# A down-projection with its operands turned around: tokens stationary, W2 moved in rows of 512 columns

## What is computed

```python
def swiglu(h, w1, w3, w2):
    return (jax.nn.silu(h @ w1) * (h @ w3)) @ w2      # D_FF = 2816, D_MODEL = 1024

h = modulate(rms_norm(x, g_ffn2[i]), sh3, sc3)
x = x + 0.5 * (1.0 + gt3[:, None, :]) * swiglu(h, w1_ffn2[i], w3_ffn2[i], w2_ffn2[i])
return rms_norm(x, g_final)
```

## Time and profile before

| | us |
|---|---|
| median of three runs | 1112.61 |
| the profiled execution's own time | 1113.34 |
| its span | 1111.5 |
| PE busy | 1095.6 |
| DVE busy | 689.1 |
| ACT busy | 583.0 |
| second down-projection, first to last matmul's start | 980.65 to 1104.00 |

### The profile page before, as it was taken

How to read it: one execution, slowest core, us unless ns; L and a number is a source line. 1 busy time by engine, 2 the same in 40 slices (tenths; PEclk the granted TensorE clock), 3 DMA queues, 4 the chain that set the end, 5 groups by cost and what they waited for, 6 DMA issues and landing times.

```text
span 1111.5 us, 17533 instructions
## 1 busy us (share of the span) xinstructions
PE 1095.6 (99%) x6320; PEld 931.4 (84%) x6320; DVE 689.1 (62%) x1166; ACT 583.0 (52%) x1049; POOL 203.0 (18%) x127
## 2 busy tenths in 40 slices
PE   7999999999999999999999999999999999999997
PEld 5678888888888888877777888888899999989997
DVE  4544444444334465659887646668788888857564
ACT  4565555555445334244656655444755555545354
POOL 0055454545432341011100000023000000000000
PEclk9999999999999999999999999999999999999999
DMA  9845664566776637539999938967876666656663
GB/s 328 280 152 189 215 199 151 189 206 223 249 233 233 210 101 228 161 102 234 220 208 204 202 82 271 249 162 188 200 213 195 198 197 184 181 181 172 170 179 118
DMA packets 274613, 218.34 MB, mean 196 GB/s; under 512 B 6663, under 2 KB 263554, under 8 KB 274434
## 3 DMA queue, kind: packets, MB, share of 16 engines
q1 hardware_dynamic: 205968, 136.86, 41.9%
q10 hardware_dynamic: 48434, 54.59, 15.1%
q0 software_dynamic: 20160, 26.22, 14.1%
HBM read 211.61 MB, written 58.46 MB: 243 GB/s over the span
## 4 chain that ended last, share of the span: by engine, by line
PE 89%; DVE 5%; ACT 3%; issue 1%; DMA 1%; ACTq 1%; DVEq 0%
PE ps L449 20%; PE ps L451 19%; PE ps L450 19%; PE ps L735 5%; PE ps L737 5%; PE ps L736 5%; PE ps L1066 2%; PE ps L1068 2%; PE ps L1067 2%; PE ps L2236 2%; PE ps L2214 1%; PE ps L2201 1%; PE ps L2181 1%; PE ps L2008 1%; DVE w_lo L428 1%
## 5 line engine op out<-in xcount | busy, mean ns | idle before, releaser
L428 DVE TENSOR_TENSOR w_lo<-raw,w_hi 128x1024 fp32r<-128x1024 f32 (+1 forms) x112 | 168.6, 1506 | 222.9 <-ACT w_hi L423 222.8
L449 PE MATMUL ps<-h_hi,w_hi 128*128 128x512 f32 x720 | 286.4, 398 | 2.3 <-DVE h_lo L515 2.0
L451 PE MATMUL ps<-h_hi,w_lo 128*128 128x512 f32 x720 | 281.0, 390 | 0.0
L450 PE MATMUL ps<-h_lo,w_hi 128*128 128x512 f32 x720 | 280.6, 390 | 0.0
L423 ACT ACTIVATE w_hi<-raw 128x1024 fp32r<-128x1024 f32 (+1 forms) x112 | 123.5, 1104 | 203.3 <-PE ps L451 193.4
L449 PEld LDWEIGHTS ps<-h_hi,w_hi 128*128 128x128 f32 x720 | 135.2, 188 | 38.2 <-issue 7.6
L451 PEld LDWEIGHTS ps<-h_hi,w_lo 128*128 128x128 f32 x720 | 135.1, 188 | 29.0
L450 PEld LDWEIGHTS ps<-h_lo,w_hi 128*128 128x128 f32 x720 | 135.4, 188 | 26.1 <-issue 0.2
L2755 POOL TENSOR_TENSOR ada<-ada 128x1024 f32<-128x1024 f32 x28 | 67.2, 2401 | 227.4 <-ACT ada L1681 227.4
L1681 ACT ACTIVATE ada<-ada,c_act 128x256 f32<-128x256 f32 x224 | 92.2, 495 | 0.0
L449 PE MATMUL ps<-g_hi,w_hi 128*128 128x512 f32 x176 | 69.3, 393 | 0.2 <-issue 0.2
(11 more groups left out here) (354 smaller groups left out, 2304.4 us busy)
## 6 DMA issues: line engine op xcount, KB each, us to landing
ada<-in_w_ada ACTq DMA_DIRECT2D x27, 1024.0 KB, 5.1
raw<-in_w_ffn SPq DMA_DIRECT2D x24, 1024.0 KB, 5.5
w_s<-in_w_ffn ACTq DMA_DIRECT2D x8, 2304.0 KB, 14.3
s_raw<-w_s SPq DMA_DIRECT2D x72, 256.0 KB, 3.2
raw<-in_w_in SPq DMA_DIRECT2D x64, 256.0 KB, 8.6
raw<-in_w_ffn SPq DMA_DIRECT2D x8, 1408.0 KB, 10.2
w_s<-in_w_ffn POOLq DMA_DIRECT2D x4, 2304.0 KB, 38.7
w_s<-w_s POOLq DMA_DIRECT2D x4, 2304.0 KB, 33.3
```

Of the source, the lines that this page charges most:

```text
L428: nc.vector.tensor_tensor(tiles_of(w_lo[j % SPL], nk), raw_of(f, j, nk), tiles_of(w_hi[j % SPL], nk).bitcast(F32), ALU.subtract).then_inc( ...
L449: nc.tensor.matmul(ps[:, bank, :], hi, rhs_hi, start=start, stop=False)
L450: nc.tensor.matmul(ps[:, bank, :], hi, rhs_lo, start=False, stop=False)
L451: return nc.tensor.matmul(ps[:, bank, :], lo, rhs_hi, start=False, stop=stop)
```

## The change

The down-projection is turned around. The gated activations are the stationary operand, 128 tokens at a time, and a row block of W2 (one f tile x 512 output channels) is the moving one, so a result is token-major: 128 tokens x 512 channels in one bank.

- DQ is 9: f tiles 4 to 12 are paired with 13 to 21, and only f tiles 0 to 3 are multiplied in the ordinary way, in three parts (std1: four token tiles, channels 0 to 511; std2: token tiles 0 and 1, channels 512 to 1023; std3: token tiles 2 and 3, the same channels, added on top of s4).
- W2 comes in 75 blocks of 128 x 512 (`BLOCKS`), in rings of four buffers. A product block serves two token tiles: six matmuls.
- `w2_sum` tensors have 1152 rows instead of 896. `gated_diff` runs for all nine quads; the ninth leaves its t2 and t4 in SBUF. The spilled x comes back in two halves of 1 MB; PE transposes it. The row 0.5 (1 + gt3) is written to DRAM (`o_row`, from the 128 x 8 tile) ahead of x_spill and read back as a broadcast over the partitions, as is g_final.
- DVE combines the products in `out_tok` in 1024-column operations (`dve_collect`, `dve_scale`). ACT squares with an accumulated sum per token, so PE makes no sums and no `fin` exists. SP writes the output in six DMAs.

```diff
-DQ = 7
+DQ = 9
-STD_F = (0, 1, 2, 3, 11, 12, 20, 21)
+STD_F = (0, 1, 2, 3)
...
+        BLOCKS = [(name, q) for name in ("std1", "std2") for q in range(len(STD_F))]
+        BLOCKS += [(name, q) for name in ("a", "s1", "s2", "d", "s3", "b", "s4") for q in range(DQ)]
+        BLOCKS += [("std3", q) for q in range(len(STD_F))]
...
+        def block_d_hi(act, n):
+            act.wait_ge(raw_in[n % 4], 32 * ROUNDS_MIX + 16 * (n // 4 + 1))
+            if n < 4:
+                act.wait_ge(prod_done, number(("d", "d", "b", "s3")[n], QUADS - 1, 1))
+            else:
+                act.wait_ge(unit_done, done(U_DOWN[1] + n - 4))
+            nc.scalar.activation(hi_d[n % 4][:, :], raw_d[n % 4][:, :], ACT.Copy).then_inc(hi_done, 1)
...
+        def pe_passes(bank, hi, lo, n, start, stop, more=False):
+            w, w_low = hi_d[n % 4][:, :], lo_d[n % 4][:, :]
+            nc.tensor.matmul(ps[:, bank, :], hi, w, start=start, stop=False, skip_group_check=more)
+            nc.tensor.matmul(ps[:, bank, :], lo, w, start=False, stop=False, skip_group_check=more)
+            return nc.tensor.matmul(ps[:, bank, :], hi, w_low, start=False, stop=stop, skip_group_check=more)
...
+        def pe_product(pe, name, q, banks, fresh):
+            n = block_at(name, q)
+            t_hi, t_lo = gated_of(name)
             pe.wait_ge(lo_done, split(U_DOWN[1] + n))
+            for i in range(2):
+                last = pe_passes(banks[i], t_hi[:, q, i * P:(i + 1) * P], t_lo[:, q, i * P:(i + 1) * P], n,
+                                 fresh and q == 0, q == DQ - 1, not fresh)
+            last.then_inc(unit_done, 1)
...
+        def pe_x(tiles, banks):
+            for i, t in enumerate(tiles):
+                for k in range(BL):
+                    last = nc.tensor.transpose(ps[:, banks[i], k * P:(k + 1) * P], xb[:, k, t * P:(t + 1) * P], ident[:, :])
+            last.then_inc(xtok_psum, 1)
...
+            for i in range(2):                       # dve_down2, after the last block
+                dve.wait_ge(unit_done, done(U_DOWN[1] + block_at("std3", i)))
+                nc.vector.tensor_tensor(last_y[i][:, :], ps[:, i, :], out_scale[:, D2], ALU.mult).then_inc(comb_done, 1)
+                dve.wait_ge(comb_done, step_d(f"last{i}"))
+                nc.vector.tensor_tensor(out_tok[:, 2 + i, D2], out_tok[:, 2 + i, D2], last_y[i][:, :], ALU.add).then_inc(comb_done, 1)
...
             sp.wait_ge(x_done, 3 * KD)
+            sp.dma_start(o_row.rearrange("(d p) -> p d", p=P), o_mul[:, 2, :], allow_slow_non_contiguous=True).then_inc(kept, 16)
             sp.dma_start(x_spill, xT[:, :, :]).then_inc(kept, 16)
...
+            elif n == 3:                             # load_d
                 sp.wait_ge(kept, 16 * (DQ + 1))
+            else:
+                sp.wait_ge(lo_done, split(U_DOWN[1] + n - 4))
...
+                if n == 7:                           # sp_down, behind load n
+                    sp.dma_start(q2_raw[:, 0:DQ - 1, :], t_spill[:, :, 0, :]).then_inc(t_back, 16)
+                if n == 10:
+                    sp.dma_start(q4_raw[:, 0:DQ - 1, :], t_spill[:, :, 1, :]).then_inc(t_back, 16)
...
+                if n == block_at("s3", 4):
+                    sp.wait_ge(xtok_psum, 2)
                     x_again(1)
```

More of the change, by code:

```diff
@@ L942, in sets @@
                 step(eng, QUADS - 1, m)
[L944 to L984, removed]
-                return
[L986 to L990, removed]
-            else:
-                act.wait_ge(unit_done, done(U_DOWN[1] + n - 3))
-            w = slice(0, piece_cols(n))
-            nc.scalar.activation(hi_d[n % 3][:, w], raw_d[n % 3][:, w], ACT.Copy).then_inc(hi_done, 1)
@@ L1058, in pe_product @@
-        def pe_product(pe, name, p, bank, fresh):
-            n = piece(name, p)
-            pe.wait_ge(lo_done, split(U_DOWN[1] + n))
-            t_hi, t_lo = gated_of(name)
-            dst = ps[:, bank, 0:HS]
-            for kk in range(DQ):
-                hi, lo = [w[n % 3][:, kk * P:(kk + 1) * P] for w in (hi_d, lo_d)]
-                nc.tensor.matmul(dst, hi, t_hi[:, kk, :], start=fresh and kk == 0, stop=False, skip_group_check=not fresh)
-                nc.tensor.matmul(dst, hi, t_lo[:, kk, :], start=False, stop=False, skip_group_check=not fresh)
-                last = nc.tensor.matmul(dst, lo, t_hi[:, kk, :], start=False, stop=kk == DQ - 1, skip_group_check=not fresh)
-            last.then_inc(unit_done, 1)
@@ L1071, in pe_std @@
-        def pe_std(pe, h, p, row):
-            n, bank = piece(h, p, row), STD_BANK[p][row]
-            pe.wait_ge(lo_done, split(U_DOWN[1] + n))
-            for i, kk in enumerate((0, 1, 2, 3) if h == "h0" else (0, 2, 1, 3)):
-                if p < 2 and h == "h1" and i % 2 == 0:
-                    pe.wait_ge(qglo_done, QUADS - 1 + i // 2)
-                k = STD_F[kk + 4 * (h == "h1")]
-                hi, lo = [w[n % 3][:, kk * P:(kk + 1) * P] for w in (hi_d, lo_d)]
-                last = passes(bank, hi, lo, g_hi[:, k, :], g_lo[:, k, :], h == "h0" and i == 0, h == "h1" and i == 3)
+        D1, D2 = slice(0, SEQ), slice(SEQ, D_MODEL)
@@ L1425, in sp_down @@
[L1425 to L1432 removed]
+                sp.wait_ge(lo_done, split(U_DOWN[1] + n - 4))
+            if name in STD_PART:
+                f, c0 = STD_F[q], 0 if name == "std1" else SEQ
+                src = w2_ffn2[0][f * P:(f + 1) * P, c0:c0 + SEQ]
+            else:
+                if name == "s1" and q == 0:
+                    sp.wait_ge(s1_summed, 80)
+                src = (w2_sum[name] if name in w2_sum else down_quarter(name))[q * P:(q + 1) * P, :]
@@ L1433, in sp_down, with x_again @@
+            sp.dma_start(raw_d[n % 4][:, :], src).then_inc(raw_in[n % 4], 16)
+        def sp_down(sp):
+            def x_again(half_):
+                sp.dma_start(xb[:, :, :], x_spill[:, BL - BL * half_:KD - BL * half_, :]).then_inc(x_back[half_], 16)
+            for n in range(len(BLOCKS)):
+                load_d(sp, n)
                 if n == 2:
-                    sp.wait_ge(prod_done, number("s1", QUADS - 1, 1))
-                    x_again(0)
+                    sp.wait_ge(t_step, 4 * DQ)
+                    sp.dma_start(t_spill[:, DQ - 2], t_out[:, :, :]).then_inc(kept, 16)
```

661 lines of the change are left out of this document (300 added, 361 removed).

## The result

The changed kernel takes 1122.88 us (median of four runs, 1120.02 to 1124.38), the kernel before 1112.83 beside it: a ratio of 1.0086, 95% interval 1.0066 to 1.0107. It is slower; the forecast was 1103.6 with a range of 1101 to 1108.

The account below looks back on a forecast made before the run. PE was taken as the bound (busy 99% of the span, 89% of the chain). Terms -6.8 matmuls, -4.4 other PE work and old waits, +1.0 new waits, +0.3 elsewhere, +0.9 tail gave -9.0: 1103.6 us, range 1101 to 1108.

Parts of the forecast that it names:

- Matmuls, -6.8: Down-projection on PE: 474 matmuls of 512 columns at 0.227 us take 107.6 us instead of 114.4.
- Rival 4: Down-projection: 512-column matmuls miss 0.227 us with W2 moving, or each block's head costs a 0.1 restart; 1110 us, chance 0.03.
- Other PE work and old waits, -4.4: Down-projection on PE: of 7.6 us of waits and small work 4.4 go; sums leave PE, x's transposes take 3.2.
- New waits, +1.0: Down-projection: PE waits for W2 blocks' low parts, DVE being late around a, s1 and s2; 1.0 us, ends 0 and 4.
- the load has 2.6 us more than the ring needs: Down-projection block loads: where DVE is on time, this slack covers whole-tile loads delaying the next by 1.3 to 2.9 us.
- rival 1: DVE and ACT become the bound from a to s2; waits of some 4 to 5 us, 1107 us, chance 0.13.
- rival 2: The ring of raw_d's four buffers is the bound, block by block, once landings pass 3.9 us; kernel slower, chance 0.07.
- Elsewhere, +0.3: Before the down-projection: larger W2 sums and o_row's write cost 0.3 us; some 3 us if both delays came through.
- o_row's write: Ahead of x_spill, before the up-projection: 1024 elements, no row pricing such a write, 11.4 us of cover behind it.
- Rival 3: In front of the up-projection, larger last sum and o_row delays reach PE: up to 11 us, 1106 to 1114, chance 0.04.
- the 11 us of cover: Before the up-projection: x_spill lands at 783.2 us and its space is wanted at 794.56, leaving 11.4 us.
- Tail, +0.9: After PE's last matmul start: 8.4 us to the span's end instead of 7.5; ends 0 and 2.

Follow-up runs that it names:

- e12: Changed kernel with W2 sums of 7 row blocks, no write of o_row, and down-projection row loads moved later: 1105.81 us, 0.9939 of the kernel before.
- e3: Changed kernel with W2 sums of 7 row blocks and no write of o_row: 1107.26 us, 0.9948 of the kernel before.
- e15: Changed kernel with copies early, first two sums apart, row loads moved, and o_row written at 982 us in ACT's queue: 1115.57 us, ratio 1.0022.
- e2: Changed kernel without the write of o_row, the output scale read from g_final instead: 1116.64 us, 1.0033 of the kernel before.
- e9: Kernel before with o_row's write of 1024 elements added in front of x_spill, read by nothing: 1115.87 us, ratio 1.0025.
- e5: Changed kernel with POOL's four W2 sums issued after the first quad of the up-projection sets: 1140.48 us, 1.0256 of the kernel before.
- e6: Changed kernel with the four W2 copies issued by POOL behind the sums of W1 and W3, not by ACT from 670 us: 1121.16 us, ratio 1.0078.
- e10: Changed kernel with the sum for s3 issued only after s1's landed and three W_out output tiles were added: 1121.70 us, ratio 1.0078.

## Why the prediction was wrong

- **Matmuls, -6.8: right.** In the changed kernel 43 starts stand between 1097.69 and 1107.21, 9.52 / 42 = 0.227. The 216 ns of the Trainium skill, TensorE: Matmul & The Clock Gate, Back-to-back issue gap, which that section gives for the isolated gap of one matmul, do not hold for this form here either. Rival 4 is dead.
- **Other PE work and old waits, -4.4: right.** In e12, without waits, first to last start is 1093.87 - 980.12 = 113.75; my terms give 107.4 (one matmul less, to its start) + 1.4 + 3.2 = 112.0. The other 1.7 are small gaps for which the trace names no releaser.
- **New waits, +1.0: too small.** The waits on lo_d are 3.0 us in sum, within its ends of 0 to 4, and the stretch is 117.9 in the changed kernel and 113.75 in e12: 4.1 with what comes behind the waits. They stand at the end of a, the start of s1 and at std3. e12, with two rows and x loaded later, has none, e3 2.2; in the versions that compute the whole with these loads moved, 0.9 to 2.5 us stayed, but for e15 with its 6.4. The step at fault is "the load has 2.6 us more than the ring needs": 4 MB in five whole-tile loads within 12 blocks are no single delay of 1.3 to 2.9. DVE and ACT (rival 1) are not the bound: in e12, with the same work on both, PE has no wait. A ring that is late throughout (rival 2) is not there either; raw_d's loads land in 2.7 and 3.4 us.
- **Elsewhere, +0.3: this is the step that failed.** It was 14.1 us. I wrote that copies and first sums run "where each unit has four loads in flight and PE shows no wait", and counted only the last sum (and that one too low: 17.5 us is the median of two, the last took 21.5 before and 29.2 in the changed kernel). No wait is not a measure of cover. The load at 706.9 already took 17.3 us of some 19.5, and the pair of sums beside it grew from 24.9 to 32.7, 1.31 times, for rows that are 9 / 7 = 1.29 as many. 17.3 x 1.3 = 22.5 would have said 3 us of wait from rows of the kernel before. With the sums alone, e2 is 9.4 over e3.
- **o_row's write, in the same step: sized by its bytes.** 4 KB of single elements take 17.2 us, and in e9 they doubled x_spill's time. Rival 3 named the mechanism, "if o_row's write held the spill as long again", but put the time at 1106 to 1114. e9 shows that the write did so (26.4 against 12.9) and used up the 11 us of cover, and that it also held loads that were issued ahead of it, which rival 3 did not reckon with. The 0.04 I gave it rested on that cover alone. The rule that I cited without a price (the Trainium skill, DMA: Bandwidth & Descriptors, Rules for kernel authors: a non-contiguous last dim becomes one descriptor per element) was the warning; the runs give the price.
- **Tail, +0.9: nearly right**, +0.5 (8.0 against 7.5; I had 8.4).
- **Half clock: missing.** After the waits of 4.3 and 2.3 us PE ran at the lower level for some 3 us: the 7 matmuls from 746.36 to 749.46 took 3.1 us instead of 1.6, the 9 from 793.57 to 797.21 took 3.6 instead of 2.0. I priced no wait with it. These 3.1 us, with the 7.8 of waits on w_lo and the 1.7 and 0.7 at 816 and 819, make 13.3 of the 14.1.

With both upstream costs gone and the loads moved (e12), the span is 1101.9 where I had 1102.5 and the median 1105.8 where I had 1103.6. The change's own stretch went as worked out; what it does to the transfers 200 us earlier decided the sign.

Left open: what in the write of single elements holds other transfers, and how much of e5's 17.6 each sum makes. The Trainium skill, DMA: Bandwidth & Descriptors, Queues, rings and completion order, says that each DMA engine takes its queues in turn, a whole packet at a time; whether that is what holds a load for 24 us beside two sums, no run here shows.

## What to carry to other kernels

A background transfer that grows is priced by the landing times of the loads beside it and by what their ring covers, not by busy shares or by the absence of waits: take the slowest such load, scale it, and compare. When one wait is taken away upstream, the next transfer in line may take its place (e6, e10), so the schedule has to be moved as a whole. And a write with a stride of one element is to be counted in elements: if a value must reach all partitions, a matmul of ones does it without touching the queues.

## What the runs showed of the hardware

- A DMA of 1024 separate 4-byte elements from SBUF to DRAM lands after 11.3 us (ACT's queue, engines idle) to 23.1 us (SP's, beside a sum), and transfers beside it land late, in its own queue or in another. Behind it in the same queue x_spill took 26.4 instead of 12.9; in other queues W_in's load, issued 2.1 us ahead of it, took 20.5 (8.9 is the median of its kind in the changed kernel), a t_spill write 7.4 instead of 3.4 and a block load 7.6 instead of 3.1.
- Two accumulating transfers of 2304 KB, DRAM to DRAM, issued together land after 19.1 and 32.7 us; of 1792 KB, 14.7 and 24.9. Alone in e10 they take 18.5 and 16.5. While the pair of 2304 KB runs, a load of 256 KB of W_out takes up to 24 us.
- Copies of 2304 KB by POOL, queued behind other sums at 612 us, took 41 to 64 us to land and PE had no wait until 709. With the same bytes copied by ACT at 670 us, beside W_out's loads, PE waited 0.7 us at 711.
